# Second block of a two-block model: the weight tiles of the rotary keys and of the gates and index weights as one tile

## The chip, the core and the metric

The kernel runs on one core of a Trainium2 chip. The metric is the device time of one execution in microseconds (us). The engines are named as in the profile: PE (TensorE, its weight loads are PEld), DVE (VectorE), ACT (ScalarE), POOL (GpSimd), SP (SyncE, which only issues DMAs here).

## The reference

The model is a first block (two layers of attention with adaptive norms and a gated feed-forward) and then a second block, in which the change lies. The second block has two layers (called layer 0 and layer 1 below) over 256 tokens of width 1024. Each takes one wide product and cuts it into the inputs of three branches:

```python
IN_WIDTHS = (DSA_Q_WIDTH,        # 512  dq
    DSA_KV_RANK,                 # 128  ckv, the latent keys and values
    ROPE_DIM,                    # 16   kr, the rotary key
    IDX_HEADS * IDX_DIM,         # 256  iq
    IDX_DIM,                     # 64   ik
    IDX_HEADS,                   # 4    iw, the weights of the index heads
    ... )                        # mi and mf, the gates of the recurrent branch, have 4 columns each
h = rms_norm_2(x, norm_w)
p = h @ w_in
k_rope = partial_rope(k_rope, cos, sin)
q_cat = jnp.concatenate([q_abs, q_rope], axis=-1).astype(jnp.float32) * DSA_HEAD_DIM ** -0.5
kv_cat = jnp.concatenate([c_kv, k_rope], axis=-1).astype(jnp.float32)
logits = jnp.einsum('bthf,btkf->bthk', qb, kv_sel)
```

So the logits of the first branch are a product over the 128 latent columns plus a product over the 16 rotary ones. Everything is in float32.

## The kernel before, in words

**Weights as a stream.** All weights lie in device memory as 504 pieces of 128 x 1024 float32 (512 KB), in the order of their use. A piece is loaded by SP into one of `SLOTS` = 7 places of `raw`. A piece holds 8 blocks of 128 x 128: the weights of one output tile of 128 features over the 8 parts of the inner dimension of 1024. The text names a piece by its slot number in the stream.

**Splitting.** PE works in a fast float32 mode of lower precision, so every operand is cut into a high and a low part. For weights this is the step `split`: ACT copies the piece to `high` (L1378), and DVE (L1778) or POOL (L1712) computes `low = raw - high`. `high` and `low` have `PAIRS` = 4 places each; a split waits until PE has used up the piece that held its place four splits ago. Each block then takes three matmuls (`product`, L984 to L986) with the split activations: high x high, high x low, low x high.

**Who subtracts.** The splits are numbered in order. `pool_share` says which go to POOL: `(1, 4)` from the start of a second block layer until its step `token("SV")`, that is every split whose number is divisible by 4; `(0, 1)`, none, in the rest.

**The order of work.** A Python program (`walk`) writes one list of steps, and every engine runs through its own part of this list in order. `fill(n)` or `some(pieces, n)` puts n pieces of matrix work (a `lin` step: one block, three matmuls) between the steps of a norm, so that PE has work while DVE, ACT and POOL do the norm.

**The start of a layer of the second block** (`second`). The products X (6 tiles) and DQ (4 tiles) are taken of the unnormed activations `U`, so that they can run before the norm's root is known. X0 is `ckv`, X1 `ik` twice, X2 `kr` and 48 zero columns twice, X3 the gates `mi`, `mf` (4 columns each, 28 zeros behind each) and `iw` (4 columns, 60 zeros), X4 and X5 `iq`; DQ0 to DQ3 are `dq`. 9 pieces of them run before the step `mean`, then 16 (layer 1: 9) before `bcast`, then 6 behind each of the 8 steps `norm`; what is left runs behind the last `norm`, and SQ0 (the next projection, which reads the normed activations `h`) comes after. A finished tile waits in one of five PSUM banks for the step `early_out`, in which DVE multiplies it by the root (L1794 for X, L1796 for DQ); at most two of these are put behind each `norm`. The norm itself: DVE scales a part k (L1951, `norm`), ACT rounds it to its high part (L1507), DVE subtracts (L1969, `normlo`). SQ0 reads all eight parts, the last matmuls the part 7.

Behind it come the norm of `ckv` (`mean` L1884 on DVE, a power on POOL L1721, three small operations, `bcast` on PE L1109, `hscale` L1984), in layer 0 the step `block2` (a memset L2092 on DVE that ACT waits for before it issues two DMAs), then eight `rope` steps of four DVE operations each (L2007 to L2013), in layer 0 each with a step `keep` (L1957), with the tiles of SQ and SK between them, and then `token("SV")`: 8 steps of six matmuls of 512 columns (L984 to L986, `bank<-high,h`), each piece of the stream for two of them.

**Where X2 is read.** In `latent` (L1265): for each pair of heads and each half of the tokens, the rotary part of the query (64 rows of `DQS`) times the 64 rows of `X[l][:, 2, :]`, of which 16 are not zero.

Of the kernel before, what the change touches and what calls it, by code (L numbers as in the profile page):

```python
# [6 lines left out]
P = 128  # L7
# [76 lines left out]
class Order:  # L84
# [3 lines left out]
    def __init__(self, plain, total, source=None):  # L88
# [6 lines left out]
        self.steps, self.filling = [], []  # L95

# [31 lines left out]
    def prepare(self, most=None):  # L128
# [3 lines left out]
        while self.next_split < self.total and most != 0:  # L132
            n = self.next_split
            if n not in self.plain:
# [11 lines left out]
                self.released.add(n)  # L146
                self.reload()
# [27 lines left out]
    def linear(self, stage, layer, j, evac=None, last=False):  # L175

        blocks = BLOCKS[stage]
        for k in range(blocks):
# [7 lines left out]
            if k == blocks - 1:  # L186
                self.hold = self.hold or last
                self.swept(self.sweeps)
                if evac:
                    evac(j)  # L190
            yield
# [77 lines left out]
def order_of_work(plain, total):  # L269
    return walk(Order(plain, total, walk(Order(plain, total)).source))  # L270


def walk(o):
# [197 lines left out]
    def second(l):  # L471

        sums, m, out = ("nw", 1) if l else ("nf", 0), ("nw", l), []
        def outer(stage):
# [3 lines left out]
                       *(o.linear("X", l, j, outer("X")) for j in range(2, 6)),  # L478
# [218 lines left out]
def psum_banks(steps):  # L697
# [13 lines left out]
    for s in steps:  # L711
# [3 lines left out]
        elif kind == "lin" and s[4] == 0:  # L715
            bank[s[:4]] = turn("acc")
        elif kind == "tok" and s[4] == 0:
# [59 lines left out]
def build(nc, plain, stream, consts, consts2, vectors, uk, uv, x_in, ctx_in, out):  # L777
# [6 lines left out]
    with ExitStack() as ctx:  # L784
# [186 lines left out]

        def split_done(slot):
            return "lo_" + work.lo_engine[slot], work.lo_no[slot]


        def tensor_program():
# [43 lines left out]
            for step in steps:  # L1020
# [227 lines left out]
                elif kind == "latent":  # L1248
# [109 lines left out]
        def scalar_program():  # L1358
# [10 lines left out]
            for step in steps:  # L1369
                kind, key = step[0], step[1:]  # L1370

                if kind == "split":
                    slot = key[0]
                    i = work.split_no[slot]
                    act.wait_ge(*arrival(slot))
# [324 lines left out]
        def gpsimd_program():  # L1700
# [4 lines left out]
            for step in steps:  # L1705
                kind, key = step[0], step[1:]

                if kind == "split" and work.lo_engine[key[0]] == "pool":
# [3 lines left out]
                    tt(low[:, i % PAIRS, :], raw[:, slot % SLOTS, :], high[:, i % PAIRS, :].bitcast(F32),  # L1712
                       ALU.subtract).then_inc(S["lo_pool"], 1)
# [23 lines left out]
        def sync_program():  # L1737
# [3 lines left out]
            for n in range(stream.shape[0]):  # L1741
                before = n - SLOTS
                if before >= 0:
                    if before in work.split_no:
# [6 lines left out]
        def vector_program():  # L1751
# [19 lines left out]
            for step in steps:  # L1771
                kind, key = step[0], step[1:]

                if kind == "split" and work.lo_engine[key[0]] == "dve":
# [3 lines left out]
                    tt(low[:, i % PAIRS, :], raw[:, slot % SLOTS, :], high[:, i % PAIRS, :].bitcast(F32),  # L1778
                       ALU.subtract).then_inc(S["lo_dve"], 1)
# [8 lines left out]
                elif kind == "early_out":  # L1788
# [4 lines left out]
                    if stage == "X":  # L1793
# [695 lines left out]
```

## Time and profile before

| What | us |
|---|---|
| median of three runs (lowest, highest) | 1940.91 (1937.87, 1942.68) |
| the profiled execution | 1936.59 |
| its span, from the first to the last instruction | 1935.1 |

The profiled execution is 4.32 us faster than the median of the runs, and 1.49 us of it lie outside the span. Times in the rows are counted from the start of the span. `xN` behind a row says how many instructions stand in it; the number in brackets is the idle time of the engine just before, and who ended it. Layer 0 of the second block begins its X tiles at 1238.49 us, layer 1 at 1584.23 us.

### The profile page before, as it was taken

What the parts mean: (1) busy time and instruction counts of PE and PEld (TensorE: products, weight loads), DVE (VectorE), ACT (ScalarE), POOL (GpSimd) and SP (SyncE); (2) the same over time, 40 slices, a digit from 0 to 9 for tenths busy, and PEclk for the clock granted to TensorE, in tenths of its full rate; (3) what the DMA queues carried; (4) which work ended last, traced back from release to release, by engine and by line L of the source; (5) the groups of instructions that cost most, each with busy time, mean ns of one, the idle gap of its engine ahead of it and who ended that gap; (6) DMA issues with size and microseconds to landing.
All of it is one profiled execution on the core that took longest, in us unless ns stands there. A gap on an engine that the chain in (4) does not pass through costs nothing.

```text
span 1935.1 us, 30478 instructions
## 1 busy us (share of the span) xinstructions
PE 1846.1 (95%) x12330; PEld 1550.5 (80%) x12330; DVE 1084.0 (56%) x2138; ACT 871.4 (45%) x1518; POOL 331.4 (17%) x158
## 2 busy tenths in 40 slices
PE   6999999999999999998999999988999999899998
PEld 2765576786888888775788999987888999788897
DVE  4335655535111111246877656788755787875576
ACT  3314444524221222243565544546555554655553
POOL 0230222342444443330000000020001001000100
PEclk9999999899999999998999999999999999999999
DMA  9343411225322322354136655554333465443342
GB/s 347 137 157 114 153 56 58 74 97 220 108 93 93 100 96 94 129 212 174 67 99 230 209 196 194 177 172 139 134 120 123 150 192 169 137 137 120 122 151 77
DMA packets 76731, 272.26 MB, mean 141 GB/s; under 512 B 8240, under 2 KB 11568, under 8 KB 76592
## 3 DMA queue, kind: packets, MB, share of 16 engines
q1 hardware_dynamic: 74656, 266.37, 40.5%
q10 hardware_dynamic: 1936, 3.94, 0.6%
q8 instruction: 98, 1.61, 0.3%
q14 instruction: 41, 0.34, 0.1%
HBM read 269.23 MB, written 1.05 MB: 140 GB/s over the span
## 4 chain that ended last, share of the span: by engine, by line
PE 75%; DVE 12%; ACT 7%; issue 3%; POOL 1%; DMA 1%; ACTq 0%; SPq 0%; DVEq 0%
PE bank L984 22%; PE bank L985 20%; PE bank L986 20%; DVE low L1778 4%; ACT high L1378 2%; PE bank L1068 2%; PE bank L1133 2%; PE bank L1164 2%; PE bank L1146 2%; POOL few L1721 1%; DMA raw<-stream 1%; DVE tmp L2250 1%; PE bank L1259 1%; DVE hx L2122 1%; PE bank L1097 0%
## 5 line engine op out<-in xcount | busy, mean ns | idle before, releaser
L984 PE MATMUL bank<-h,high 128*128 128x256 f32 (+1 forms) x2208 | 713.6, 323 | 15.5 <-DVE h L1974 3.4
L985 PE MATMUL bank<-h,high 128*128 128x256 f32 (+1 forms) x2208 | 689.3, 312 | 0.0
L986 PE MATMUL bank<-h,low 128*128 128x256 f32 (+1 forms) x2208 | 688.8, 312 | 0.0
L1378 ACT ACTIVATE high<-raw 128x1024 fp32r<-128x1024 f32 x408 | 427.3, 1053 | 229.3 <-PE bank L986 224.4
L984 PEld LDWEIGHTS bank<-h,high 128*128 128x128 f32 x2208 | 418.8, 190 | 94.1 <-issue 53.1
L1778 DVE TENSOR_TENSOR low<-raw,high 128x1024 fp32r<-128x1024 f32 x287 | 357.1, 1250 | 158.7 <-ACT high L1378 157.8
L986 PEld LDWEIGHTS bank<-h,low 128*128 128x128 f32 x2208 | 418.3, 189 | 26.1
L985 PEld LDWEIGHTS bank<-h,high 128*128 128x128 f32 x2208 | 418.5, 190 | 23.3
L1712 POOL TENSOR_TENSOR low<-raw,high 128x1024 fp32r<-128x1024 f32 x121 | 292.4, 2422 | 548.6 <-ACT high L1378 548.6
L1721 POOL TENSOR_TENSOR few<-few,halves 128x2 f32<-128x2 f32 (+2 forms) x27 | 26.9, 998 | 703.3 <-DVE few L1884 703.3
L1822 DVE TENSOR_TENSOR gt<-bank,gt 128x512 f32<-128x512 f32 (+1 forms) x44 | 24.5, 557 | 189.9 <-PE bank L986 187.5
L984 PE MATMUL bank<-hid,high 128*128 128x512 f32 (+1 forms) x352 | 117.1, 333 | 0.0
L986 PE MATMUL bank<-hid,low 128*128 128x512 f32 (+1 forms) x352 | 117.1, 333 | 0.0
L985 PE MATMUL bank<-hid,high 128*128 128x512 f32 (+1 forms) x352 | 117.1, 333 | 0.0
L1816 DVE SCALAR_TENSOR_TENSOR xc<-bank,mod,xc 128x256 f32<-128x256 f32 x72 | 32.6, 481 | 142.7 <-PE bank L986 142.6
L1068 PE MATMUL bank<-raw,silu_c 128*32 128x512 f32 x384 | 88.1, 626 | 15.5 <-DMA raw<-stream 15.4
L1567 ACT ACTIVATE hid<-gt 128x512 fp32r<-128x512 f32 (+1 forms) x44 | 23.1, 525 | 137.8 <-DVE gt L1822 137.8
L984 PEld LDWEIGHTS bank<-hid,high 128*128 128x128 f32 x352 | 66.1, 188 | 6.9
L985 PEld LDWEIGHTS bank<-hid,high 128*128 128x128 f32 x352 | 66.1, 188 | 6.8
L986 PEld LDWEIGHTS bank<-hid,low 128*128 128x128 f32 x352 | 66.1, 188 | 6.8
L1733 POOL TENSOR_TENSOR z<-z,dqs 128x1024 f32<-128x1024 f32 x2 | 6.2, 3111 | 342.6 <-ACT dqs L1646 342.6
L2029 DVE TENSOR_REDUCE small<-bank 128x1 f32<-128x512 f32 (+1 forms) x96 | 54.7, 598 | 17.5 <-PE bank L1133 16.0
(304 smaller groups left out, 2742.5 us busy)
## 6 DMA issues: line engine op xcount, KB each, us to landing
raw<-stream SPq DMA_DIRECT2D x504, 512.0 KB, 3.4
xc<-x_in SPq DMA_DIRECT2D x1, 1024.0 KB, 5.8
xc<-ctx_in SPq DMA_DIRECT2D x1, 1024.0 KB, 8.0
cst<-consts ACTq DMA_DIRECT2D x1, 896.0 KB, 6.0
cst<-consts ACTq DMA_DIRECT2D x1, 704.0 KB, 4.1
ukw<-uk ACTq DMA_DIRECT2D x1, 512.0 KB, 5.1
uvw<-uv ACTq DMA_DIRECT2D x1, 512.0 KB, 7.1
out<-xc ACTq DMA_DIRECT2D x1, 512.0 KB, 2.9
```

The source lines that it names most:

```text
L984: mm(dst, wh, xh, start=start, stop=False)
L985: mm(dst, wh, xl, start=False, stop=False)
L986: return mm(dst, wl, xh, start=False, stop=stop)
L1068: ins = mm(banks[b][g, :], silu_c[:, k, :], raw[:, block // BLK % SLOTS, at:at + 512], start=k < 4, stop=k >= 4)
L1133: mm(banks[b][:, 0:w], Q[l][head(g), 4 * b_ + j, t * P:(t + 1) * P], K[l][head(g), b_, keys], start=True, stop=True).then_inc(S["S"], 1)
L1146: ins = nc.tensor.transpose(banks[b][:, s * P:(s + 1) * P], p[:, s * P:(s + 1) * P], ident)
L1164: ins = mm(banks[7][head(g), j * P:(j + 1) * P], V[l][:, first + s, c:c + HD], probT[l][2 * (i % LAG[l]) + g][:, s * P:(s + 1) * P], start ...
L1378: do(high[:, i % PAIRS, :], raw[:, slot % SLOTS, :], ACTF.Copy).then_inc(S["hi"], 1)
L1712: tt(low[:, i % PAIRS, :], raw[:, slot % SLOTS, :], high[:, i % PAIRS, :].bitcast(F32), ALU.subtract).then_inc(S["lo_pool"], 1)
L1721: tt(f[:, 8:8 + w], f[:, 0:w], halves[:, 0:w], ALU.pow).then_inc(S["pow"], 1)
L1778: tt(low[:, i % PAIRS, :], raw[:, slot % SLOTS, :], high[:, i % PAIRS, :].bitcast(F32), ALU.subtract).then_inc(S["lo_dve"], 1)
L2029: nc.vector.tensor_reduce(st[:, g:g + 1], ps[:, 0:w], AX.X, ALU.max, negate=True).then_inc(S["masked_max"], 1)
```

## The change

The tiles X2 and X3 become one. Both pieces of the stream are still loaded (slots 318 and 319 in layer 0, 412 and 413 in layer 1), but they are split together into one place of `high` and `low`: of each block the columns 0 to 95 from the second piece (gates and index weights), the columns 96 to 127 from the first (16 rotary columns and 16 zeros). ACT and the subtracting engine take two instructions for it. PE does 8 steps `lin` fewer in each layer, into one bank. `early_out` for X2 takes rows 96 to 127 of this bank and writes them to rows 0 to 31 and 64 to 95 of `X[l][:, 2, :]`, after two memsets of the other rows. `latent` reads 32 rows in place of 64. The counts of pieces put between the steps (9, 16 or 9, 6) stay.

```diff
@@ class Order
+        self.joined = set(joined)
...
             n = self.next_split
+            if n in self.joined:
+                self.next_split += 1
+                continue
             if n not in self.plain:
...
                 self.released.add(n)
+                if n - 1 in self.joined:
+                    self.released.add(n - 1)
                 self.reload()
...
+    def joint(self, stage, layer, j, evac=None):
+        first = self.at // BLK
+        if self.draft:
+            self.joined.add(first)
+        for i in range(2):
+            self.take()
+            self.at += BLK
+        for k in range(BLK):
+            self.split_by_now(first + 1)
+            self.block_of[stage, layer, j + 1, k] = (first + 1) * BLK + k
+            if k == BLK - 1:
+                self.sweeps += 1
+                self.sweep_of[stage, layer, j] = self.sweep_of[stage, layer, j + 1] = self.sweeps
+            self.step("lin", stage, layer, j + 1, k)
+            if k == BLK - 1:
+                self.swept(self.sweeps)
+                for i in range(2):
+                    evac(j + i)
+            yield
@@ def second(l)
         pieces = chain(o.together([("X", l, j) for j in range(2)], outer("X")),
-                       *(o.linear("X", l, j, outer("X")) for j in range(2, 6)),
+                       o.joint("X", l, 2, outer("X")),
+                       *(o.linear("X", l, j, outer("X")) for j in range(4, 6)),
                        *(o.linear("DQ", l, j, outer("DQ")) for j in range(4)))
@@ def build
+        def sources(slot):
+            at = slot % SLOTS, work.split_no[slot] % PAIRS
+            if slot - 1 not in work.joined:
+                return [(raw[:, at[0], :], high[:, at[1], :], low[:, at[1], :])]
+            of = lambda t, i, c: t[:, i, :].rearrange("p (b c) -> p b c", c=P)[:, :, c]
+            own, added, beside = slice(0, 96), slice(96, P), slice(0, 32)
+            return [(of(raw, at[0], own), of(high, at[1], own), of(low, at[1], own)),
+                    (of(raw, (slot - 1) % SLOTS, beside), of(high, at[1], added), of(low, at[1], added))]
@@ tensor_program, latent
-                                ins = mm(banks[bg][:, c], DQS[l][head(g), hd // 2, t * P:(t + 1) * P],
-                                         X[l][head(g), 2, 0:(t + 1) * P], start=False, stop=t == 1)
+                                turned = slice(HD * g, HD * g + 32)
+                                ins = mm(banks[bg][:, c], DQS[l][turned, hd // 2, t * P:(t + 1) * P],
+                                         X[l][turned, 2, 0:(t + 1) * P], start=False, stop=t == 1)
@@ scalar_program, split
-                    do(high[:, i % PAIRS, :], raw[:, slot % SLOTS, :], ACTF.Copy).then_inc(S["hi"], 1)
+                    for w, h, _ in sources(slot):
+                        ins = do(h, w, ACTF.Copy)
+                    ins.then_inc(S["hi"], 1)
@@ vector_program, split (and the same in gpsimd_program)
-                    tt(low[:, i % PAIRS, :], raw[:, slot % SLOTS, :], high[:, i % PAIRS, :].bitcast(F32),
-                       ALU.subtract).then_inc(S["lo_dve"], 1)
+                    for w, h, lo in sources(slot):
+                        ins = tt(lo, w, h.bitcast(F32), ALU.subtract)
+                    ins.then_inc(S["lo_dve"], 1)
@@ vector_program, early_out
-                    if stage == "X":
+                    if stage == "X" and j == 2:
+                        nc.vector.memset(X[l][32:64, 2, :], 0.0)
+                        nc.vector.memset(X[l][96:128, 2, :], 0.0)
+                        tt(X[l][0:32, 2, :], ps[96:128, :], rs[96:128, :], ALU.mult)
+                        tt(X[l][64:96, 2, :], ps[96:128, :], rs[96:128, :], ALU.mult).then_inc(S["drained_dve"], 1)
+                    elif stage == "X":
                         tt(X[l][:, j, :], ps, rs, ALU.mult).then_inc(S["drained_dve"], 1)
```

The joined split is one split, so every split behind it has a number lower by one in layer 0, and by two in layer 1 behind its own joined split. With `pool_share` (1, 4) other pieces go to POOL. In layer 0 these are the slots 320, 324, 328, 332, 336 before and 321, 325, 329, 333, 337 with the change; in layer 1 the slots 416, 420, 424, 428 before and 414, 418, 422, 426, 430 with it. On each engine the instructions stand as follows (the same line of code has a number that is 43 to 55 higher in the changed file).

DVE, layer 0, from the second step `norm` (tmp<-xc; h<-tmp,h is `normlo`, x<-bank,lat is `early_out`), before:

```order
L1951 SCALAR_TENSOR_TENSOR tmp<-xc,small,bank 128x256
L1969 TENSOR_TENSOR h_1<-tmp,h_0 128x256
L1778 TENSOR_TENSOR low<-raw,high 128x1024
L1794 TENSOR_TENSOR x<-bank,lat 128x256 x2
L1951 SCALAR_TENSOR_TENSOR tmp<-xc,small,bank 128x256
L1969 TENSOR_TENSOR h_1<-tmp,h_0 128x256
L1794 TENSOR_TENSOR x<-bank,lat 128x256
L1951 SCALAR_TENSOR_TENSOR tmp<-xc,small,bank 128x256
```

The same place with the change:

```order
L2006 SCALAR_TENSOR_TENSOR tmp<-xc,small,bank 128x256
L2024 TENSOR_TENSOR h_1<-tmp,h_0 128x256
L1828 TENSOR_TENSOR low<-raw,high 128x1024
L1844 MEMSET x 32x256
L1845 MEMSET x 32x256
L1846 TENSOR_TENSOR x<-bank,lat 32x256
L1847 TENSOR_TENSOR x<-bank,lat 32x256
L1849 TENSOR_TENSOR x<-bank,lat 128x256
L2006 SCALAR_TENSOR_TENSOR tmp<-xc,small,bank 128x256
L2024 TENSOR_TENSOR h_1<-tmp,h_0 128x256
L1849 TENSOR_TENSOR x<-bank,lat 128x256 x2
L2006 SCALAR_TENSOR_TENSOR tmp<-xc,small,bank 128x256
```

One of the two `x<-bank,lat` ahead of the third `norm` has become four operations, and ahead of the fourth `norm` two of them now stand in place of one.

POOL, from the end of layer 0's work (`z<-z,dqs`) to that of layer 1, before (few<-few is the power of a norm):

```order
L1721 TENSOR_TENSOR few<-few,halves 128x2 x5
L1712 TENSOR_TENSOR low<-raw,high 128x1024 x3
L1721 TENSOR_TENSOR few<-few,halves 128x2
L1712 TENSOR_TENSOR low<-raw,high 128x1024
L1733 TENSOR_TENSOR z<-z,dqs 128x1024
```

and with the change:

```order
L1770 TENSOR_TENSOR few<-few,halves 128x2 x4
L1761 TENSOR_TENSOR low<-raw,high 128x1024
L1770 TENSOR_TENSOR few<-few,halves 128x2
L1761 TENSOR_TENSOR low<-raw,high 128x1024 x2
L1770 TENSOR_TENSOR few<-few,halves 128x2
L1761 TENSOR_TENSOR low<-raw,high 128x1024 x2
L1782 TENSOR_TENSOR z<-z,dqs 128x1024
```

A subtraction of a whole piece now stands ahead of the power of layer 1's first norm, and ahead of the second power (that of the norm of `ckv`) there are two where there were three.

DVE, layer 1, from the small operations of its first norm, before:

```order
L1893 SCALAR_TENSOR_TENSOR few<-few 128x2
L1778 TENSOR_TENSOR low<-raw,high 128x1024 x2
L1951 SCALAR_TENSOR_TENSOR tmp<-xc,vec,bank 128x256
L1794 TENSOR_TENSOR x<-bank,lat 128x256 x2
L1951 SCALAR_TENSOR_TENSOR tmp<-xc,vec,bank 128x256
L1969 TENSOR_TENSOR h_1<-tmp,h_0 128x256
L1794 TENSOR_TENSOR x<-bank,lat 128x256
```

and with the change:

```order
L1948 SCALAR_TENSOR_TENSOR few<-few 128x2
L1828 TENSOR_TENSOR low<-raw,high 128x1024 x2
L2006 SCALAR_TENSOR_TENSOR tmp<-xc,vec,bank 128x256
L1828 TENSOR_TENSOR low<-raw,high 128x1024
L1849 TENSOR_TENSOR x<-bank,lat 128x256 x2
L2006 SCALAR_TENSOR_TENSOR tmp<-xc,vec,bank 128x256
L2024 TENSOR_TENSOR h_1<-tmp,h_0 128x256
L1844 MEMSET x 32x256
```

A third subtraction of a piece has come between the first and the second `norm`; before, POOL did that one. On PE 48 matmuls have gone, 24 in each layer, and the rest stands in the order of before.

## Rows read from the trace of the kernel before

**Rows 1.** The page: busy time of each engine; the chain by engine.

```profile
PE 1846.1 (95%) x12330; PEld 1550.5 (80%) x12330; DVE 1084.0 (56%) x2138; ACT 871.4 (45%) x1518; POOL 331.4 (17%) x158
...
PE 75%; DVE 12%; ACT 7%; issue 3%; POOL 1%; DMA 1%; ACTq 0%; SPq 0%; DVEq 0%
```

**Rows 2.** Busy time in two stretches: us, PE, PEld, DVE, ACT, POOL, PEclk, DMA share, GB/s.

```profile
1238.50:1309.00 70.50, 63.76 (x503) 60.56 (x502) 56.62 (x113) 30.94 (x46) 14.35 (x8) 1.00 0.52 172
1584.20:1648.60 64.40, 63.77 (x498) 61.31 (x496) 50.47 (x98) 30.39 (x46) 10.97 (x6) 1.00 0.52 169
```

**Rows 3.** Timeline of PE, layer 0: start, us, engine, line, operation, idle before.

```profile
1249.90 0.65 PE L1109 MATMUL bank<-cst,few 128*128 128x128 f32 x4 [1.64 <-DVE few L1923]
...
1266.05 0.28 PE L984 MATMUL bank<-U,high 128*128 128x256 f32 x1
...
1268.77 0.28 PE L984 MATMUL bank<-U,high 128*128 128x256 f32 x1
...
1271.64 0.38 PE L984 MATMUL bank<-h,high 128*128 128x256 f32 x1
...
1298.89 0.50 PE L984 MATMUL bank<-high,h 128*128 128x512 f32 x1 [2.36 <-DVE low L1778]
...
1306.39 0.51 PE L984 MATMUL bank<-high,h 128*128 128x512 f32 x1 [1.73 <-DVE low L1778]
```

**Rows 4.** Timeline of ACT, layer 0, at the same place.

```profile
1240.34 1.99 ACT L1378 ACTIVATE high<-raw 128x1024 fp32r<-128x1024 f32 x2
```

**Rows 5.** Timeline of DVE, layer 0.

```profile
1241.42 2.36 DVE L1778 TENSOR_TENSOR low<-raw,high 128x1024 fp32r<-128x1024 f32 x2 [0.27 <-ACT high L1378]
...
1246.93 2.33 DVE L1915 SCALAR_TENSOR_TENSOR few<-few 128x2 f32<-128x2 f32 x1 [0.81 <-POOL few L1726]
...
1256.14 0.75 DVE L1794 TENSOR_TENSOR x<-bank,lat 128x256 f32<-128x256 f32 x2
...
1259.97 2.27 DVE L1778 TENSOR_TENSOR low<-raw,high 128x1024 fp32r<-128x1024 f32 x1 [1.30 <-ACT high L1378]
...
1271.17 0.41 DVE L1969 TENSOR_TENSOR h<-tmp,h 128x256 fp32r<-128x256 f32 x1
...
1279.96 0.27 DVE L2092 MEMSET ones<- 4x256 f32 x1
...
1292.47 2.71 DVE L2010 SCALAR_TENSOR_TENSOR tmp<-tmp,small,cst 128x256 f32<-128x256 f32 x1
...
1305.11 4.62 DVE L1778 TENSOR_TENSOR low<-raw,high 128x1024 fp32r<-128x1024 f32 x4
```

**Rows 6.** Timeline of POOL, layer 0.

```profile
1258.76 2.40 POOL L1712 TENSOR_TENSOR low<-raw,high 128x1024 fp32r<-128x1024 f32 x1 [9.51 <-ACT high L1378]
...
1292.51 2.40 POOL L1712 TENSOR_TENSOR low<-raw,high 128x1024 fp32r<-128x1024 f32 x1 [7.56 <-ACT high L1378]
```

**Rows 7.** Timeline of DVE, layer 1.

```profile
1595.61 0.47 DVE L1951 SCALAR_TENSOR_TENSOR tmp<-xc,vec,bank 128x256 f32<-128x256 f32 x1
1596.00 2.13 DVE L1969 TENSOR_TENSOR h<-tmp,h 128x256 fp32r<-128x256 f32 x1
...
1612.83 0.41 DVE L1969 TENSOR_TENSOR h<-tmp,h 128x256 fp32r<-128x256 f32 x1
...
1620.96 0.16 DVE L1893 SCALAR_TENSOR_TENSOR few<-few 128x2 f32<-128x2 f32 x1
```

**Rows 8.** Timeline of POOL, layer 1.

```profile
1595.44 2.40 POOL L1712 TENSOR_TENSOR low<-raw,high 128x1024 fp32r<-128x1024 f32 x1 [6.37 <-ACT high L1378]
...
1617.48 2.40 POOL L1712 TENSOR_TENSOR low<-raw,high 128x1024 fp32r<-128x1024 f32 x1 [5.99 <-ACT high L1378]
```

**Rows 9.** Timeline of PE, layer 1.

```profile
1615.52 0.28 PE L984 MATMUL bank<-h,high 128*128 128x256 f32 x1
...
1621.27 0.38 PE L1109 MATMUL bank<-cst,few 128*128 128x128 f32 x2
...
1648.65 0.97 PE L1192 MATMUL bank<-x 64*128 64x128 f32 x4 [0.69 <-ACT SV L1419]
```

More of the change, by code:

```diff
@@ L84, with __init__ @@
 class Order:
-    def __init__(self, plain, total, source=None):
+    def __init__(self, plain, total, source=None, joined=()):
         self.stream_plain, self.total = sorted(plain), total
@@ L269, in order_of_work @@
 def order_of_work(plain, total):
-    return walk(Order(plain, total, walk(Order(plain, total)).source))
+    draft = walk(Order(plain, total))
+    return walk(Order(plain, total, draft.source, draft.joined))
 def walk(o):
@@ L716, in psum_banks @@
             bank[s[:4]] = turn("acc")
+            if s[1] == "X" and s[3] == 3:
+                bank["lin", "X", s[2], 2] = bank[s[:4]]
         elif kind == "tok" and s[4] == 0:
@@ L970, in arrival @@
             return f"slot{slot % SLOTS}", 16 * (slot // SLOTS + 1)
+        def sources(slot):
[6 more added lines that the diff above has]
+                    (of(raw, (slot - 1) % SLOTS, beside), of(high, at[1], added), of(low, at[1], added))]
         def split_done(slot):
+            if slot in work.joined:
+                slot += 1
             return "lo_" + work.lo_engine[slot], work.lo_no[slot]
@@ L1374, in scalar_program @@
                     i = work.split_no[slot]
+                    if slot - 1 in work.joined:
+                        act.wait_ge(*arrival(slot - 1))
                     act.wait_ge(*arrival(slot))
@@ L1711, in gpsimd_program @@
                     pool.wait_ge("hi", i + 1)
-                    tt(low[:, i % PAIRS, :], raw[:, slot % SLOTS, :], high[:, i % PAIRS, :].bitcast(F32),
-                       ALU.subtract).then_inc(S["lo_pool"], 1)
+                    for w, h, lo in sources(slot):
+                        ins = tt(lo, w, h.bitcast(F32), ALU.subtract)
+                    ins.then_inc(S["lo_pool"], 1)
                 elif kind == "mean":
@@ L1743, in sync_program @@
                 if before >= 0:
-                    if before in work.split_no:
+                    if before in work.split_no or before in work.joined:
                         sp.wait_ge(*split_done(before))
@@ L1777, in vector_program @@
                     dve.wait_ge("hi", i + 1)
-                    tt(low[:, i % PAIRS, :], raw[:, slot % SLOTS, :], high[:, i % PAIRS, :].bitcast(F32),
-                       ALU.subtract).then_inc(S["lo_dve"], 1)
+                    for w, h, lo in sources(slot):
+                        ins = tt(lo, w, h.bitcast(F32), ALU.subtract)
+                    ins.then_inc(S["lo_dve"], 1)
                 elif kind == "earlylo":
```

## The prediction

> **What bounds the kernel now.** I read the page first: PE is busy for 95% of the span and stands for 75% of the chain that ended last [rows 1]. By that alone, work taken from PE is time won. But the share is an average, so next I looked at the two stretches in which the change lies, from the first X tile to the end of `token("SV")`. In layer 1 PE is busy for 63.8 of 64.4 us: it bounds. In layer 0 it is busy for as long, but the stretch takes 70.5 us, and DVE is busy for 56.6 of them [rows 2]. There the timeline of PE shows where it stands: 1.64 us for the root of the norm, then 2.36 and 1.73 us in `token("SV")` for `low` of a piece from DVE [rows 3]. So from the norm on DVE sets the end in layer 0: between the first and the last of these waits PE only fills time.
>
> The third view is DVE beside POOL. `low` of 1024 columns costs DVE 1.2 us, but one took 2.27: it ended at 1262.24, 1.08 us after POOL's subtraction, which ran until 1261.16 [rows 5, 6]. A rope operation of 0.5 us took 2.71 and ended behind POOL's of 1292.51 as well [rows 5, 6], and so did a `normlo` in layer 1 (2.13 us), while the `norm` before it, which reads PSUM and one buffer, ran at 0.47 us in the middle of POOL's work [rows 7, 8]. So a DVE operation with two inputs in SBUF stands still while POOL subtracts a piece, for up to 2.2 us, and one with a single SBUF input doesn't. The memsets and the products of PSUM with one buffer in the new `early_out` are of the second kind, and I charge them no wait. The Trainium skill, "SBUF — State Buffer", section "Who interferes with whom", says the same: the second read port is an exclusive lock; a DVE instruction with one SBUF input doesn't need it. The trace agrees.
>
> **What the change takes away.** 24 matmuls in each layer. In layer 0, 24 of them take 1268.77 - 1266.05 = 2.72 us [rows 3]. Two layers: 5.4 us, 0.28%. That is all that PE can give back, if nothing else is in the way. It also takes one split from each layer's list: ACT's copy (1.99 / 2 = 1.0 us [rows 4]) and DVE's subtraction (2.36 / 2 = 1.18 us [rows 5]). `latent` keeps its columns, so I cost its 32 rows at nothing. Both pieces are still loaded; DMA is at about half in both stretches [rows 2], so this is hidden.
>
> **What it adds.** (1) The joined split: two instructions in place of one. On DVE 256 columns cost 0.75 / 2 = 0.375 us and 1024 cost 1.18 [rows 5], so 1.05 ns a column and 0.11 us for each instruction; 768 and 256 columns make 1.29 us, +0.11. On ACT, which shows no smaller one in my rows, +0.1 by the same measure (bounds: 0 and 0.4, a whole small operation). (2) `early_out` of X2: one operation of 0.375 us becomes two of this and two memsets. The only memset near is 0.27 us [rows 5]; between zero and 0.375 each I take 0.27. Together +0.9 us (0.4 to 1.1). (3) Each later `early_out` stands one `norm` earlier: +0.375 us ahead of the last `norm`. (4) Other pieces go to POOL.
>
> The Trainium skill speaks against such pieces: "VectorE: DVE Perf Modes", section "The TRN2 errata", has each instruction pay a fixed latency and advises at least 512 elements. Its formula of (N + 151) / 0.96 ns would price the extra ones at 0.16 for the split and about 1.2 for `early_out`, 0.3 us a layer above my sum. No row here shows operations of 32 rows.
>
> **Layer 0, step by step.** The joined split is at the head of the norm (1240.34 on ACT, 1241.42 on DVE), right on the path to the root: +0.2, PE's wait of 1.64 becomes 1.8. From the root on, DVE and ACT hand over to each other: `norm`, ACT's high part, ACT's copy of the next piece, DVE's `low`, `early_out`, `norm`. DVE's wait of 1.30 ahead of a `low` [rows 5] is of this kind, so operations between a `low` and a `norm` lengthen the chain in full: +0.9. The additional `early_out` (3) falls where DVE waits for POOL anyway (the `low` of 2.27) and is hidden; were it not, +0.375. So `normlo` of part 7, which ended at 1271.17 + 0.41 = 1271.58, ends at 1272.7. PE used it at 1271.64, almost without a wait [rows 3]. With 2.72 us less to do and +0.2 it comes at 1269.1 and waits 3.6 us. **All that PE wins in layer 0 is gone here**, and it is 1.1 us late.
>
> Behind this, DVE has one piece less to subtract ahead of `block2` (POOL has slot 329, where it had 328; 329 was DVE's): 1.1 - 1.2, so `block2` is about where it was, 1279.96 [rows 5], or 0.3 earlier. Then the new turns of POOL tell. Before, POOL subtracted 332 while DVE was waiting, and 336 in the ropes (the row of 2.71). Now it subtracts 333, inside the first ropes, a further hit of 0 to 2.2 us, I take 1.6, and 337 in the place of 336's hit. So `low` of 335, for which PE went on at 1298.89 [rows 3], comes at 1298.9 - 0.3 + 1.6 = 1300.2. Piece 336 was POOL's and came early; now it is DVE's, two pairs of `keep` and `rope` later. Three ropes and four keeps took 1305.11 - 1298.89 = 6.2 us [rows 3, 5], so two pairs take about 4.0: 1300.2 + 4.0 + 1.2 = 1305.4. A step of `token("SV")` is (1306.39 - 1.73 - 1298.89) / 4 = 1.44 us. Before, PE had two steps to do from 1306.39: end 1309.3. Now four from 1305.4 on: 1311.1. That is **+1.8 us**.
>
> **Layer 1.** Here PE bounds, and had slack: `normlo` 7 ended at 1613.24, PE wanted it at 1615.52 [rows 7, 9], 2.3 us. With 2.7 us less to do PE comes at 1612.8. DVE is later by the 0.9 of (2) and 0.375 of (3), and a piece that POOL did is its own (the third order fence), but POOL's hit on `normlo` (2.13 for 0.41: 1.7 us) goes: +0.9, 1614.1. PE waits 1.3 and keeps 1.4 us. Then comes the norm of `ckv`: its root was there at 1621.12, PE wanted it at 1621.27 [rows 7, 9]. The root must come 1.4 us earlier for PE to keep the gain. POOL's subtraction ahead of its power (1617.48, 2.40 [rows 8]) is gone from here, but POOL now does slot 422 right behind `normlo` 7 (from about 1614.6 to 1617.0), and DVE's next two pieces wait for it: 1617.0 + 1.1 + 0.4 + 1.2 = 1619.7, then the small operations and the power, 1.4 us: 1621.1. So PE is back to its old time, about 0; at best it keeps 1.4. The one for slot 414 delays the power of the first norm to 1589.5, and the root comes just in time. I take **-0.1**.
>
> **Banks.** With a tile less, the turn of the five banks shifts. In layer 1 a score waits 0.69 us for a bank that SV filled [rows 9]; with the change SV fills two others, and in layer 0 the first tile behind SV gets a free one. Bounds 0 and -1.4 (the same once more in layer 0); I take **-0.7**.
>
> **Sum.** +1.8 - 0.1 - 0.7 = +1.0 us. 1936.59 + 1.0 = 1937.6 for the execution that was profiled; this stood 4.3 us below the median of the runs, so **1941.9 us** in their terms. A difference under 0.3% (5.8 us) is about what a measurement of this kernel can't tell from none.
>
> **The rivals.**
> - *It stays as reckoned* (DVE and POOL eat PE's gain): -1.5 to +3.5 us, 1939.4 to 1944.4. Chance 0.56.
> - *Layer 1 keeps PE's gain.* If POOL's 422 ends before DVE wants to subtract, the root is early and the 2.7 us come through, with layer 0 at nothing: -2.7, 1938.2. For it speaks that PE bounds there [rows 2]; against it the slack of 0.15 us at 1621.27. Chance 0.20.
> - *PE bounds in both.* -5.4 us, 1935.5; with the one split less, 1934.5. Against it stand the three waits of layer 0. Chance 0.09.
> - *POOL's turns make it slower.* Any subtraction of POOL that meets a DVE chain on the path costs up to 2.2 us [rows 5, 6]. Five in layer 0 and five in layer 1 have new places; I have counted one further hit of 1.6. With two more full ones on the path, +1.0 + 4.4 = +5.4, 1946.3; from the third on, 1948.5, it is measurably slower. Chance 0.12.
> - *The joined tile is not cheaper at all* (the split of two pieces waits for both, the narrow copies cost more than their columns): +2, 1943. Chance 0.03.
>
> **The numbers.** Range 1936.0 to 1946.5: it leaves out the tails of the third and fourth. The likeliest case alone has 1939.4 to 1944.4. Faster by over 0.3% only if the third case comes with a split's time more: 0.06. Slower by as much: 0.09. The rest, 0.85, is within it.
>
> **What would show it.** In the changed profile: 48 matmuls less on PE; in layer 0 a wait of about 3.6 us at the eighth part of SQ0, which wasn't there, and in SV a wait of over 2 us for slot 336 ahead of the third pair of steps; memsets below 0.3 us; in layer 1 a wait at the last parts of SQ0 of about 1.3 us and one at `bcast` of about 1.4. Wrong would be: SQ0 running through in layer 0, or the X and DQ tiles of layer 1 ending 2.7 us earlier with nothing waiting behind them, or POOL's subtraction leaving rope operations at 0.5 us.

## The result and the profile after

The changed kernel takes 1944.16 us in the median of 16 runs (1939.66 to 1949.83), the kernel before 1940.43 us in 16 runs beside it (1937.61 to 1942.68). The ratio is 1.0021, 95% interval 1.0014 to 1.0028: about 4.1 us slower. That is within the 0.3% that I called no change, but the interval leaves 1 out: it is a small slowdown. The forecast was 1941.9 us, +1.0. The profiled execution took 1941.92 us with a span of 1940.5. (In the experiments below, one execution each of old_turns, drain_only and no_pool took 9616, 2618 and 5598 us and is left out of the ratios.)

The page of the changed kernel, busy time and the chain by engine:

```profile
PE 1845.4 (95%) x12282; PEld 1547.5 (80%) x12282; DVE 1086.5 (56%) x2143; ACT 871.0 (45%) x1518; POOL 333.8 (17%) x159
...
PE 75%; DVE 12%; ACT 7%; issue 2%; POOL 1%; DMA 1%; SPq 0%; ACTq 0%; DVEq 0%
```

PE has its 48 matmuls less, and yet only 0.7 us less busy time [rows 1]. The two stretches show why. They run here from the first X matmul to ACT's first drain of SV; in the same cut the kernel before has 70.98 and 63.78 us.

```profile
1240.46:1315.26 74.80, 65.85 (x482) 61.56 (x481) 58.50 (x116) 30.40 (x47) 14.41 (x8) 0.93 0.49 169
1590.39:1654.72 64.33, 61.61 (x476) 58.15 (x475) 51.15 (x100) 28.62 (x44) 13.32 (x7) 1.00 0.50 166
```

In layer 0 the stretch is 3.82 us longer and PE is busy for longer, with fewer instructions. The first of the last three columns is PE's granted clock: 0.93, where it was 1.00 [rows 2]. In layer 1 PE is busy for 2.1 us less, and 0.55 us are lost all the same. What lies outside: before the first X tile +1.97 us, where nothing is changed (in my profiles this part ends anywhere from 1238.5 to 1244.0 us), between the stretches +0.37, behind them -1.31.

PE in layer 0, timeline of the changed kernel:

```profile
1274.62 0.39 PE L1027 MATMUL bank<-h,high 128*128 128x256 f32 x1 [2.76 <-DVE h L2024]
...
1275.29 0.39 PE L1027 MATMUL bank<-h,high 128*128 128x256 f32 x1
...
1275.81 0.41 PE L1027 MATMUL bank<-h,high 128*128 128x256 f32 x1
1276.03 0.41 PE L1028 MATMUL bank<-h,high 128*128 128x256 f32 x1
...
1304.05 0.79 PE L1027 MATMUL bank<-high,h 128*128 128x512 f32 x1 [3.47 <-DVE low L1828]
1304.64 0.63 PE L1028 MATMUL bank<-low,h 128*128 128x512 f32 x1
...
1309.33 0.60 PE L1027 MATMUL bank<-high,h 128*128 128x512 f32 x1
```

Windows of the same kernel (the granted clock is the third number from the right):

```profile
1270.00:1275.00 5.00, 1.37 (x10) 0.97 (x8) 3.90 (x10) 2.10 (x4) 0.00 (x0) 1.00 0.43 117
1275.00:1280.00 5.00, 4.95 (x30) 4.75 (x29) 2.15 (x3) 2.27 (x4) 2.89 (x2) 0.66 0.39 140
1280.00:1285.00 5.00, 5.00 (x46) 5.00 (x45) 2.36 (x6) 1.45 (x3) 0.18 (x1) 1.00 0.56 183
...
1303.00:1304.00 1.00, 0.00 (x0) 0.00 (x0) 1.00 (x2) 0.00 (x0) 0.00 (x0) 0.50 0.00 0
1304.00:1309.00 5.00, 4.95 (x12) 3.80 (x12) 4.79 (x13) 0.00 (x0) 0.00 (x0) 0.50 0.30 105
```

Matmuls of 256 columns that began 0.11 us apart begin 0.21 us apart from 1275.8 on: the clock fell to 1.2 GHz about a microsecond after the wait of 2.76 us, and came back some 3.4 us later. It fell again in the wait of 3.47 us: the windows above have 0.50 from 1303, before PE starts again. It was back by about 1309.8. The kernel before waited for 2.36 and 1.73 us [rows 3] and kept 2.4 GHz. This is the part of the result that I had not foreseen.

DVE in layer 0, timeline of the changed kernel:

```profile
1257.12 1.23 DVE L1828 TENSOR_TENSOR low<-raw,high 128x1024 fp32r<-128x1024 f32 x1 [1.10 <-ACT high L1425]
1258.45 0.27 DVE L1844 MEMSET x<- 32x256 f32 x1
1258.82 0.27 DVE L1845 MEMSET x<- 32x256 f32 x1
1259.10 0.42 DVE L1846 TENSOR_TENSOR x<-bank,lat 32x256 f32<-32x256 f32 x1
1259.54 0.43 DVE L1847 TENSOR_TENSOR x<-bank,lat 32x256 f32<-32x256 f32 x1
1260.00 0.42 DVE L1849 TENSOR_TENSOR x<-bank,lat 128x256 f32<-128x256 f32 x1
...
1274.82 0.42 DVE L2024 TENSOR_TENSOR h<-tmp,h 128x256 fp32r<-128x256 f32 x1
...
1282.11 1.23 DVE L1828 TENSOR_TENSOR low<-raw,high 128x1024 fp32r<-128x1024 f32 x1 [1.34 <-ACT high L1425]
1283.25 0.47 DVE L2039 SCALAR_TENSOR_TENSOR x<-x,vec,bank 128x256 f32<-128x256 f32 x1
1283.72 0.27 DVE L2147 MEMSET ones<- 4x256 f32 x1
...
1288.37 2.71 DVE L2065 SCALAR_TENSOR_TENSOR tmp<-tmp,small,cst 128x256 f32<-128x256 f32 x1
...
1299.36 2.57 DVE L2063 TENSOR_TENSOR tmp<-dqs,cst 128x256 f32<-128x256 f32 x1
...
1302.77 1.22 DVE L1828 TENSOR_TENSOR low<-raw,high 128x1024 fp32r<-128x1024 f32 x1
...
1307.89 1.22 DVE L1828 TENSOR_TENSOR low<-raw,high 128x1024 fp32r<-128x1024 f32 x1
```

From the last `low` before X2's `early_out` to the next product DVE needs 1.73 us (its follower could start at about 1258.27), where one product needs 0.34: +1.4. `normlo` 7 ends at 1275.24, which is 34.78 us behind the first X matmul; before it was 33.09. The two rope operations of 2.71 and 2.57 us are the hits of POOL's slots 333 and 337 (a hit: a DVE operation with two inputs in SBUF that stands still while POOL subtracts). The `low` at 1282.11, of slot 331, waited for ACT's copy, and ACT for PE:

```profile
1280.74 0.38 ACT L1449 ACTIVATE dqs<-bank 128x256 f32<-128x256 f32 x1 [3.36 <-PE bank L1029]
1281.02 1.05 ACT L1425 ACTIVATE high<-raw 128x1024 fp32r<-128x1024 f32 x1
```

PE in layer 1, timeline of the changed kernel:

```profile
1620.33 0.39 PE L1027 MATMUL bank<-h,high 128*128 128x256 f32 x1 [1.64 <-DVE h L2024]
...
1627.85 0.43 PE L1152 MATMUL bank<-cst,few 128*128 128x128 f32 x2 [0.90 <-DVE few L1948]
```

### The profile page after: what moved, and what is told of

Its sections match the earlier page's. It is cut to its first block, busy times and chain, and to the rows that moved or that the text cites. A ratio compares the mean times of both kernels' runs of the same rounds, so it can differ in the third digit from the quotient of the medians.

```text
span 1940.5 us, 30386 instructions
## 1 busy us (share of the span) xinstructions
PE 1845.4 (95%) x12282; PEld 1547.5 (80%) x12282; DVE 1086.5 (56%) x2143; ACT 871.0 (45%) x1518; POOL 333.8 (17%) x159
## 4 chain that ended last, share of the span: by engine, by line
PE 75%; DVE 12%; ACT 7%; issue 2%; POOL 1%; DMA 1%; SPq 0%; ACTq 0%; DVEq 0%
PE bank L1027 22%; PE bank L1029 20%; PE bank L1028 20%; DVE low L1828 4%; ACT high L1425 3%; PE bank L1111 2%; PE bank L1207 2%; PE bank L1176 2%; PE bank L1189 2%; DMA raw<-stream 1%; POOL few L1770 1%; DVE tmp L2305 1%; PE bank L1302 1%; DVE hx L2177 1%; PE bank L1140 0%
## 5 line engine op out<-in xcount | busy, mean ns | idle before, releaser
L1828 DVE TENSOR_TENSOR low<-raw,high 128x1024 fp32r<-128x1024 f32 (+2 forms) x286 | 353.8, 1244 | 161.8 <-ACT high L1425 161.0
```

Source lines behind the costliest of these rows:

```text
L1828: ins = tt(lo, w, h.bitcast(F32), ALU.subtract)
```

## The experiments

Three theories. **A**: the new turns of POOL cost, because its subtractions meet other DVE operations. **B**: what was added on DVE costs, X2's `early_out` above all, more than its own length. **C**: POOL's stalls of DVE are worth bearing, since DVE has no time to do the pieces itself. None of them names PE's clock, which has a section of its own below.

The table gives each kernel's ratio to the kernel before, with its interval. From each one's profiled execution it gives the two stretches; for layer 0 the time from the first X matmul to the end of `normlo` 7, from there to the memset of `block2`, and from there to ACT's drain of SV; and the mean granted clock of both stretches. These are single executions, and not always typical ones: that of the change is 2.2 us below the median of its kernel, that of best 3.2 us above.

| Kernel | ratio | layer 0 | layer 1 | to normlo 7 | to block2 | to SV | clocks |
|---|---|---|---|---|---|---|---|
| before | 1 | 70.98 | 63.78 | 33.09 | 8.38 | 29.51 | 1.00, 1.00 |
| the change | 1.0021 | 74.80 | 64.33 | 34.78 | 8.48 | 31.54 | 0.93, 1.00 |
| old_turns | 1.0007 [0.9997, 1.0018] | 71.66 | 65.67 | 34.85 | 8.41 | 28.40 | 0.95, 0.97 |
| turns_only | 1.0062 [1.0046, 1.0078] | 76.58 | 68.26 | 36.76 | 6.96 | 32.86 | 0.98, 0.97 |
| before_phases | 1.0019 [1.0009, 1.0028] | 71.48 | 66.17 | 34.01 | 6.81 | 30.66 | 0.98, 0.97 |
| phase_2_1 | one run, 1943.97 us | 77.14 | 62.74 | 38.21 | 8.51 | 30.42 | 0.93, 1.00 |
| phase_3_3 | one run, 1954.6 us | 74.99 | 73.28 | 36.77 | 8.37 | 29.85 | 0.95, 0.93 |
| no_pool | 1.0047 [1.0031, 1.0062] | 75.93 | 68.41 | 37.32 | 8.94 | 29.67 | 0.91, 0.95 |
| drain_only | 1.0010 [1.0000, 1.0020] | 71.77 | 63.28 | 34.46 | 8.38 | 28.93 | 0.98, 1.00 |
| memsets_early | 1.0025 [1.0016, 1.0033] | 73.78 | 63.63 | 34.04 | 8.50 | 31.24 | 0.95, 1.00 |
| plain_split | 1.0023 [1.0013, 1.0032] | 74.55 | 64.76 | 34.62 | 8.46 | 31.47 | 0.93, 0.97 |
| bare | 0.9997 [0.9983, 1.0012] | 71.61 | 62.83 | 33.15 | 6.91 | 31.55 | 0.95, 1.00 |
| best | 0.9996 [0.9987, 1.0005] | 71.56 | 62.08 | 34.70 | 8.46 | 28.40 | 0.95, 1.00 |
| bare_best | 0.9994 [0.9985, 1.0003] | 72.05 | 61.57 | 34.27 | 8.48 | 29.30 | 0.95, 1.00 |

### The turns of POOL

**old_turns**: the change, with the slots that POOL had before.

```diff
-                e = "pool" if i % self.pool_share[1] < self.pool_share[0] else "dve"
+                turn = i + sum(m < n for m in self.joined)
+                e = "pool" if turn % self.pool_share[1] < self.pool_share[0] else "dve"
```

> The changed kernel, with the pieces that POOL subtracts put back to those of before (slots 320, 324, 328, 332, 336 and 416, 420, 424, 428). Measured from the first X tile to the drain of SV: before 70.98 us in layer 0 and 63.78 in layer 1, changed 74.80 and 64.33. Theory A (the turns of POOL cost most: 333 hits a rope, 336 falls to DVE): layer 0 falls to 71 to 72.5, layer 1 to 62 to 63.8; the whole is within 1 us of before or below it. Theory B (the four operations of early_out and the lateness of PE behind them cost most, whoever subtracts): layer 0 stays at 74 or more.

**turns_only**: the kernel before, with the slots that POOL has after the change.

```diff
+                turn = i - (n >= 319) - (n >= 413)
+                e = "pool" if turn % self.pool_share[1] < self.pool_share[0] else "dve"
```

> The kernel before, with the pieces that POOL subtracts moved to those of the changed kernel, and nothing else. Theory A: layer 0 goes from 70.98 to 73 to 74 us, the whole 2 to 4 us slower than before. Theory B: both stretches within 0.7 us of before.

The old turns take back 0.14 of the 0.21% (the two intervals just overlap, so this difference is less sure than the stretches), all of it in layer 0 (74.80 to 71.66 us); layer 1 gets worse by 1.3. The new turns alone make the kernel before slower by 0.62%, three times the whole change. A holds as to the place where the time goes, but "the new turns are bad" does not: a turn is good or bad for one order of the steps.

**phase_2_1** and **phase_3_3**: the change, `i` replaced by `i + 2` and `i + 3` in layer 0, by `i + 1` and `i + 3` in layer 1 (POOL: 319, 323, 327, 331, 335 and 417, 421, 425, 429; 322, 326, 330, 334 and 415, 419, 423, 427, 431).

> The changed kernel, with POOL's turn two splits earlier in layer 0 and one earlier in layer 1 (slots 319, 323, ... and 417, 421, ...). Theory A: the time of a stretch follows from where the subtraction of POOL falls, so both stretches move by 1 to 5 us, either way. Theory B (lateness behind the new early_out): layer 0 stays within 1 us of 74.80.

> The changed kernel, with POOL's turn three splits earlier in both layers (slots 322, 326, ... and 415, 419, ...), so that together with the runs at hand all four places are seen in layer 0. Theory A: moves of 1 to 5 us either way. Theory B: within 1 us of 74.80 in layer 0.

With the change and old_turns (which moves layer 0 by one, layer 1 by two) these make all four phases. Moved by 0, 1, 2 and 3, layer 0 takes 74.8, 71.7, 77.1 and 75.0 us, layer 1 64.3, 62.7, 65.7 and 73.3. Moved by one is best in both, by one execution each.

**no_pool**: the change, `o.pool_share = (0, 1)` in the second block too: DVE subtracts every piece.

> The changed kernel, with no piece given to POOL in the second block: DVE subtracts all. It takes away the standstills of DVE behind POOL (in the changed trace of layer 0 they add up to about 8 us: 2.2 at the root, 1.1 at a low, 2.2 and 2.2 in ropes) and adds five subtractions of 1.18 us to DVE in each layer. Theory A (what counts is how long DVE stands or works on the path): layer 0 falls below 74.80, to about 72.5 to 74, layer 1 to 62 to 64. Theory C (POOL's help is worth more than its lock costs): layer 0 grows to 76 or more, layer 1 to 66.

0.47% slower than before. `normlo` 7 comes 2.5 us later than in the change and PE waits three times at SQ0 (7.2 us in all). C holds.

### What was added on DVE

**drain_only**: the kernel before, with the four operations of the new `early_out` for X2 (the products take rows 0 to 31 of X2's own bank).

```diff
-                    if stage == "X":
+                    if stage == "X" and j == 2:
+                        nc.vector.memset(X[l][32:64, 2, :], 0.0)
+                        nc.vector.memset(X[l][96:128, 2, :], 0.0)
+                        tt(X[l][0:32, 2, :], ps[0:32, :], rs[0:32, :], ALU.mult)
+                        tt(X[l][64:96, 2, :], ps[0:32, :], rs[0:32, :], ALU.mult).then_inc(S["drained_dve"], 1)
+                    elif stage == "X":
```

> The kernel before, with early_out of X2 as two memsets and two products of 32 rows (out of the first 32 rows of its own tile), and nothing else. Theory A: layer 0 grows by 0 to 1.4 us (the 1.4 us that the new early_out took more in the changed trace), layer 1 by nothing, since normlo had 2.3 us of slack there. Theory B: layer 0 grows by 2.5 us or more.

`normlo` 7 comes 1.37 us later, which is the price of the four operations in the chain of the norm (the split is untouched here). At the end of layer 0 +0.79 of it is left; the whole costs 0.10%, just at the edge of its interval.

**memsets_early**: the change, with both memsets ahead of the first power of the norm, where DVE waits for POOL.

> The changed kernel, with the two memsets of X2 taken out of early_out and put where DVE waits for the power of the norm, so that early_out of X2 is two operations. Two memsets took 0.7 us of the path in each layer. Theory A: layer 0 falls from 74.80 by about 0.7 us, since the chain of DVE and POOL behind it is as it was. Theory B (lateness is fed back and grows): it falls by 1.4 us or more.

`normlo` 7 comes 0.74 us earlier: the memsets are half of the 1.4. The stretches are 1.0 and 0.7 us shorter, but the ratio is not lower than the change's: so small a gain can't be told in the whole.

**bare**: the change, with the joined piece split by one instruction each (of the second piece alone), X2's `early_out` one product of one column, and its memset early. The rotary keys are left out of the computation. **plain_split**: of this only the plain split; the four operations stay.

```diff
-            if slot - 1 not in work.joined:
+            if True:
                 return [(raw[:, at[0], :], high[:, at[1], :], low[:, at[1], :])]
```

> The changed kernel without what the joining adds: the joined piece is split as a plain one (one instruction each), and early_out of X2 is one product of one column, with a memset of the whole tile where DVE waits for the power. The rotary keys are left out of the computation by this. POOL's turns are those of the changed kernel. Theory A: layer 0 falls from 74.80 by the added work on the path, 1.4 + 0.2 us, to about 73, still above the 70.98 of before. Theory B: it falls by 3 us or more, to 71 to 72, layer 1 to below 62.

> The change, with the joined split made by one instruction on ACT and one on DVE, of the second piece alone (the rotary keys are left out of the computation: X2 gets other columns); the four operations of X2's early_out stay, POOL's turns are those of the change. It parts what the bare kernel took away. If the cost is in X2's early_out (my prediction's term of 0.9 against 0.2 for the split), the stretches stay near the change's, at least 74.3 and 64.0 us against 74.80 and 64.33. If the two-part split costs more than its columns and delays the root of the norm, layer 0 falls to about 73.5 or below, and the first wait at bcast falls from 1.8 to under 1.5.

Plain_split stands where the change stands (1.0023 beside 1.0021); the wait at `bcast` falls from 1.80 to 1.6 us, the 0.2 that I had charged. So the split is cheap, and what bare gains (0.24%) comes with `early_out`. B holds, with more than its length: `normlo` 7 is 1.63 us earlier, but the stretch is 3.19 shorter. The other 1.57 lie between `normlo` 7 and `block2`, where both kernels have the same steps and the same turns.

### The clock

Bare and memsets_early differ nowhere in this part either, and PE waited nearly as long in both, 2.46 and 2.49 us. PE of bare, then of memsets_early:

```profile
1274.84 0.39 PE L1027 MATMUL bank<-h,high 128*128 128x256 f32 x1 [2.46 <-DVE h L2024]
...
1276.65 0.28 PE L1027 MATMUL bank<-h,high 128*128 128x256 f32 x1
1276.77 0.28 PE L1028 MATMUL bank<-h,high 128*128 128x256 f32 x1
1276.88 0.28 PE L1029 MATMUL bank<-h,low 128*128 128x256 f32 x1
```

```profile
1274.89 0.38 PE L1027 MATMUL bank<-h,high 128*128 128x256 f32 x1 [2.49 <-DVE h L2026]
...
1276.71 0.38 PE L1027 MATMUL bank<-h,high 128*128 128x256 f32 x1
1276.89 0.41 PE L1028 MATMUL bank<-h,high 128*128 128x256 f32 x1
1277.10 0.41 PE L1029 MATMUL bank<-h,low 128*128 128x256 f32 x1
```

In one the clock stays, in the other it falls. ACT's copy of the next weight piece waits for SQ1's end on PE. It began 4.83 us after PE's restart in bare (1279.67):

```profile
1279.39 0.38 ACT L1449 ACTIVATE dqs<-bank 128x256 f32<-128x256 f32 x1 [1.89 <-PE bank L1029]
1279.67 1.05 ACT L1425 ACTIVATE high<-raw 128x1024 fp32r<-128x1024 f32 x1
```

and 6.42 us after it in memsets_early:

```profile
1281.03 0.38 ACT L1449 ACTIVATE dqs<-bank 128x256 f32<-128x256 f32 x1 [3.48 <-PE bank L1029]
1281.31 1.05 ACT L1425 ACTIVATE high<-raw 128x1024 fp32r<-128x1024 f32 x1
```

That is 1.59 us, and the way from `normlo` 7 to `block2` is 6.91 us in bare and 8.50 in memsets_early, 1.59 more. DVE pays it, since its next `low` stands ahead of `hscale` and `block2`.

The other kernels bear this out. Where DVE has two `low` on this way, it takes 6.81 to 6.96 us without a fall at SQ0 (bare, turns_only, before_phases) and 8.41 to 8.50 with one (the change, memsets_early, plain_split, old_turns, best, bare_best). No_pool, phase_2_1 and phase_3_3 wait a second time at SQ0 behind the fall and don't compare (8.94, 8.51, 8.37). The kernel before and drain_only have a third `low` there and no fall: 8.38. So the change does save one subtraction of DVE here, and the fall eats what it saves. It is the fall and not the wait: turns_only waited for 3.61 us at SQ0, longer than any of those six (2.49 to 3.57 us), kept its clock, and has 6.96. PE of turns_only:

```profile
1278.27 0.39 PE L985 MATMUL bank<-h,high 128*128 128x256 f32 x1 [3.61 <-DVE h L1970]
1278.49 0.28 PE L986 MATMUL bank<-h,high 128*128 128x256 f32 x1
...
1280.02 0.28 PE L987 MATMUL bank<-h,low 128*128 128x256 f32 x1
```

So a fall at SQ0 costs about 1.6 us on this way. That the additions bring the fall isn't shown: in one profiled execution each, it came behind 2.49 us and not behind 2.46.

Drain_only shows the shortest wait with a fall behind it:

```profile
1302.15 0.50 PE L984 MATMUL bank<-high,h 128*128 128x512 f32 x1 [1.90 <-DVE low L1778]
1302.49 0.39 PE L985 MATMUL bank<-low,h 128*128 128x512 f32 x1
...
1303.72 0.63 PE L984 MATMUL bank<-high,h 128*128 128x512 f32 x1
1304.15 0.63 PE L985 MATMUL bank<-low,h 128*128 128x512 f32 x1
```

The Trainium skill, "TensorE: Matmul & The Clock Gate", section "Part 1: The HAM clock gate (the "warmup" mystery)", says that a gate lets through either half or all of the pulses, by how busy the engine has lately been, and that its observation runs free of the kernel. The trace agrees with the two levels: starts 0.11 or 0.21 us apart and nothing lasting between. That two waits that differ by 0.03 us end differently fits the free-running observation, but doesn't show it.

### The best turns

**before_phases**: the kernel before, with turns moved by one in both layers (319, 323, 327, 331, 335 and 415, 419, 423, 427, 431). **best**: the change, with `i + 1` in both layers (320, 324, 328, 332, 336 and 417, 421, 425, 429) and the memsets early. **bare_best**: bare with the turns of best; the rotary keys are left out here too.

```diff
+                turn = i + (1 if n < 400 else 1)
+                e = "pool" if n > 314 and turn % self.pool_share[1] < self.pool_share[0] or n <= 314 and i % self.pool_share[1] < self.pool_share[0] else "dve"
```

> The kernel before with POOL's turns moved by one split in both layers (POOL has 319, 323, 327, 331, 335 and 415, 419, 423, 427, 431), the fair opponent of the change at its own best turns. If the turns of the kernel before were as good as they can be by chance (A), it is slower, by 1 to 8 us. If they were not, it is level or faster, and then nothing of a gain of the change at its best turns is the change's own.

> The change, with X2's two memsets ahead of the norm's first power and POOL's turns moved by one split in each layer (POOL has 320, 324, 328, 332, 336 and 417, 421, 425, 429). If the place of POOL's subtractions and the added operations are two causes that add (A and B), the stretches should be about 71.66 - 1.0 = 70.7 us in layer 0 and 62.74 - 0.7 = 62.0 in layer 1 (before: 70.98 and 63.78), and the execution about 2 us faster than the kernel before: ratio 0.9985 to 0.9995, the first kernel with the change to be no slower at all. If the two are one (what the memsets gave in the change was only that they stood beside the same stall of POOL), the stretches stay at 71.7 and 62.7 and the ratio at 1.000.

> The bare kernel (joined piece split by one instruction, X2's early_out one product of one column, its memset early; the rotary keys are left out of the computation) with the turns of the best kernel. It bounds what the change could give if its additions were free and POOL stood well. If PE's matmuls were the bound once DVE is relieved, both stretches fall by PE's 2.72 us and more: 68.3 and 61.1, ratio 0.997. If DVE's chain with ACT still sets the end in layer 0, it stays above 69.5 there and only layer 1 gains: ratio 0.998 to 0.999.

The `normlo` of old_turns and that of best:

```profile
1259.16 1.46 DVE L2025 TENSOR_TENSOR h<-tmp,h 128x256 fp32r<-128x256 f32 x1
```

```profile
1260.44 2.18 DVE L2027 TENSOR_TENSOR h<-tmp,h 128x256 fp32r<-128x256 f32 x1
```

Best is level with the kernel before, and a quarter of a per cent better than the change as it was made. In layer 1 the two causes add (62.08 us; 62.0 expected), in layer 0 they don't (71.56 against old_turns' 71.66): a `normlo` behind X2's `early_out` meets POOL's subtraction in both. It took 1.46 us in old_turns and 2.18 in best, 0.72 more: what the memsets gave is gone in it. Bare_best is no better (0.9994): with free additions and good turns, layer 0 still takes 72.05 us. Beside bare it gains 2.25 us behind `block2`, but loses 1.12 ahead of `normlo` 7, where POOL now stops two subtractions of DVE (2.25 and 2.22 us) in place of one (2.24), and 1.57 to a fall of the clock behind a wait of 3.57 us at SQ0. The kernel before, moved by one turn, is slower by 0.19%, and with the turns of the change by 0.62%, so its own turns were good ones for its order.

## Why the prediction was right, and where not

The class (a change under 0.3%) and the range were right. The likeliest time was 2.3 us too low in the median, and the sum (+1.0) about 3 us short of the difference. Part of this was luck. By the difference, +4.1 us by the ratio or +3.7 by the medians, the result lies outside the -1.5 to +3.5 of the likeliest case. Its 1944.16 us lie inside 1939.4 to 1944.4 only since the kernel before, too, came out lower in 16 runs (1940.43) than in the three that the forecast starts from (1940.91).

- **PE can give back 2.72 us a layer, and in layer 0 all of it is waited away.** Right. PE waits for 0.87 and 2.76 us at SQ0, 3.63 together; 3.6 was said (all of it at the eighth part, where the trace has some at the part before).
- **The joined split, +0.2.** Right: `bcast` 1.80 us, as said, and 1.6 with the plain split.
- **`early_out` of X2, +0.9 (0.4 to 1.1).** Too small, and outside its bounds: +1.4 by the rows, 1.37 by drain_only. The durations of the memsets were right (0.27 each), the products took 0.42 and 0.43 where I had 0.375. I had let them overlap as a pair of wide products does (0.75 us for two); these and the next one start 0.37, 0.28, 0.44 and 0.46 apart, the first 0.18 late. The estimate by the formula of the Trainium skill, "VectorE: DVE Perf Modes", section "The TRN2 errata", was nearer: three operations more of (256 + 151) / 0.96 ns make 1.27 us (the prediction says about 1.2). The products agree with it (0.42 and 0.43 us), the memsets don't (0.27); the page has the formula for an addition of two tensors. That POOL doesn't hold them up isn't tested in the change, where POOL subtracts until 1251.37 and again from 1262.29. Old_turns bears it out for a product: it took 0.43 us from 1257.97 on, with POOL subtracting from 1257.92.
- **`normlo` 7, +1.1 us.** +1.69, by the term above.
- **"So `block2` is about where it was, 1279.96, or 0.3 earlier".** This is the step that failed. It was 1.8 us later than before, 2.1 later than I said: 0.6 by `normlo` 7 and 1.5 by the way from there. I took a wait of 3.6 us on PE to cost its own length alone; behind it PE ran at 1.2 GHz, the bank of SQ1 came free later, and ACT and then DVE waited for it. That DVE has one piece less here was right. Bare, where the clock stayed, has 6.91 us for this way, and turns_only 6.96; by my numbers it was 1279.66 - 1272.7 = 6.96.
- **From `block2` to the end of `token("SV")`.** 31.54 us; my steps came to 31.4 (1311.1 - 1279.66). POOL's 333 hit the ropes (2.2 us; I took 1.6), 337 as well. The wait of over 2 us for slot 336 doesn't show: the two steps ahead of it ran at 1.2 GHz, 5.28 us for twelve matmuls in place of 2.88, and used it up. Without the fall PE would have stood from 1306.9 to the end of that `low`, 1309.1.
- **Layer 1, -0.1.** +0.55. The waits were said to be 1.3 and 1.4 us and are 1.64 and 0.90. (For the first I had added up +0.9 us; 0.9 + 0.375 + 1.2 - 1.7 makes +0.8.) The place of each was right, and with it that POOL's 422 stops DVE's next piece (2.58 us). The two waits and 2.72 us of work less make 63.6; 0.7 us more were taken. Most of them stand in PE's busy time, which fell by 2.13 us and not by 2.72; why isn't shown.
- **Banks, -0.7.** A score behind layer 1's SV waits 0.26 us where it was 0.69 [rows 9]; outside the two stretches and the start the change is 0.9 us faster. How much of this the banks make isn't shown.
- **The waits of PE before.** I named three in layer 0. A fourth, of 1.01 us at 1278.50 for the root of the norm of `ckv`, was left out; it speaks for DVE as the bound, too.
- **The rivals.** "POOL's turns make it slower" was the real danger: turns_only shows 12 us, for the kernel before. I gave it 0.12 with a price for two further hits, 4.4 us; over the four phases layer 0 spreads by 5.5 us and layer 1 by 10.5.

So the changed parts give 3.82 + 0.55 - 0.94 = +3.4 us, the ratio 4.1 (2.7 to 5.4). Two causes make it, and either one taken away brings the kernel to about level: the turns (old_turns, 1.0007) or the additions (bare, 0.9997). Both away give hardly more (0.9994). Their prices don't add in layer 0: bare gains all of its time ahead of `block2` (1.63 us to `normlo` 7, 1.57 by the clock), old_turns behind it (3.14 us), but bare_best loses part of it again, ahead of `normlo` 7 and to the clock, as said above.

Only one execution of each kernel has a profile, but the mean granted clock of the whole span is on record for each. In the 16 of the change it was 0.982 to 0.986, in 32 of the kernel before 0.985 to 0.989: PE ran at 1.2 GHz for longer in general, and not in the profiled one alone. The runs of the changed kernel spread over 10.2 us and those of the kernel before over 5.1. The clock doesn't explain that spread: the slowest run (1949.83 us) had 0.985, the fastest (1939.66) 0.984. What does stays open, and no kernel was tried that keeps PE busy through the wait at SQ0.

## What to carry to other kernels

Work taken from PE is time won only where PE sets the end; elsewhere it turns into a wait, and the wait can cost more than its length, because the matmuls behind it may run at half the clock and the engines that wait for PE's buffers inherit that. Price an operation of few rows on DVE like one of 128, and don't let it overlap. When a change renumbers pieces that are dealt out in turn, try the turns anew before judging the change, and give the kernel before the same chance.

## What was not expected of the hardware

- PE's clock fell after a wait of 1.90 us in drain_only, stayed at 2.4 GHz after one of 2.36 us in the kernel before [rows 3], stayed after 2.46 us in bare and fell after 2.49 in memsets_early. In turns_only it stayed after 3.61 us at SQ0 and after 3.48 us in SV, where the change lost it in one of 3.47. The length of the last wait alone doesn't tell it.
- A memset of 32 rows and 256 columns took 0.27 us on DVE, as one of 4 rows does [rows 5], and a product of 32 rows 0.42 to 0.43, as one of 128 rows (0.42).
